# A mixture-of-experts down projection in wide passes: transposed columns and turning them back, or 128 rows and 32-token strips; and the order of the experts

## The reference, cut to what matters

```python
logits = (xf @ router_w) + router_b
top_val, top_idx = lax.top_k(logits, TOP_K)          # 4 of 32 experts
gates = jax.nn.softmax(top_val, axis=-1)
...
h = xb @ w1 + b1                                      # w1[e]: 1024 x 2048
x_glu = jnp.minimum(h[..., :D_FF], 7.0)
x_lin = jnp.clip(h[..., D_FF:], -7.0, 7.0)
act = x_glu * jax.nn.sigmoid(1.702 * x_glu) * (x_lin + 1.0)
return act @ w2 + b2                                  # w2[e]: 1024 x 1024
...
y = einsum("tk,tkd->td", gates, y_assign)             # out = h + y
```

## Time and profile before

| | us |
|---|---|
| runs | 1978.64, 1984.21, 1984.33 |
| median | 1984.21 |
| span of the profiled execution, first to last instruction | 1979.4 |
| TensorE busy in it | 1920.4 |
| prologue, to the first matmul of the first pass | 444.5 |
| 18 narrow passes (n = 128) | 771.2 |
| 14 wide passes (3 of 136, 5 of 144, 3 of 152, 2 of 176, 1 of 192) | 745.9 |
| from the last matmul to the end | 17.8 |

### The profile page before, as it was taken

One profiled execution on the slowest core, in us unless ns is written; L12 is line 12 of the kernel. 1 busy time (PEld: TensorE's weight loads), 2 busy tenths in 40 slices (PEclk: granted clock), 3 DMA queues, 4 the chain that ended last, 5 costly groups with the idle time before them and its releaser, 6 DMA issues.

```text
span 1979.4 us, 34969 instructions
## 1 busy us (share of the span) xinstructions
PE 1920.4 (97%) x12847; PEld 1585.1 (80%) x12848; DVE 1008.8 (51%) x2627; ACT 450.0 (23%) x983; POOL 397.5 (20%) x410
## 2 busy tenths in 40 slices
PE   5999999989999999999999999999999999999996
PEld 3555555458888778888877888999999999999996
DVE  2989983455555455555545555444444444443332
ACT  3166584121111111111111111221222121111111
POOL 3111100012222212212221212222222222221211
PEclk9999999999999999999999999999999999999998
DMA  7000035348999999999999999998888889887651
GB/s 243 1 1 1 10 108 198 127 146 317 344 334 351 340 352 353 344 332 353 341 350 352 351 339 331 324 322 308 303 301 301 301 291 310 306 294 250 220 178 40
DMA packets 237155, 513.10 MB, mean 259 GB/s; under 512 B 11121, under 2 KB 15757, under 8 KB 237104
## 3 DMA queue, kind: packets, MB, share of 16 engines
q1 hardware_dynamic: 215408, 448.89, 62.9%
q0 software_dynamic: 19840, 63.09, 11.8%
q10 hardware_dynamic: 1856, 0.41, 0.1%
HBM read 479.30 MB, written 33.05 MB: 259 GB/s over the span
## 4 chain that ended last, share of the span: by engine, by line
PE 93%; DVE 3%; ACT 1%; issue 1%; DMA 1%; POOL 0%; SPq 0%; ACTq 0%; DVEq 0%; POOLq 0%
PE bank L1178 50%; PE bank L1222 12%; PE bank L1197 12%; PE bank L1395 6%; PE bank L1270 4%; DVE arena L934 2%; PE bank L1306 2%; PE bank L1317 1%; PE bank L1210 1%; PE bank L1211 1%; PE bank L1345 1%; DMA arena<-in_x 1%; PE bank L1564 0%; PE bank L1262 0%; PE bank L1420 0%
## 5 line engine op out<-in xcount | busy, mean ns | idle before, releaser
L1178 PE MATMUL bank<-arena 128*128 128x128 f32 (+5 forms) x8192 | 999.1, 283 | 7.0 <-issue 6.1
L1178 PEld LDWEIGHTS bank<-arena 128*128 128x128 f32 x8192 | 984.9, 191 | 18.9 <-issue 17.7
L379 POOL DMA_INDIRECT arena<-token_rows,idx_q x256 | 246.7, 964 | 667.9 <-PE bank L1178 624.4
L810 DVE TENSOR_SCALAR arena<-bank,b1c 128x256 f32<-128x256 f32 x256 | 123.4, 482 | 404.2 <-PE bank L1178 404.2
L499 ACT ACTIVATE arena<-arena 128x256 f32<-128x256 f32 x256 | 106.6, 417 | 849.1 <-DVE arena L810 849.1
L1222 PE MATMUL bank<-arena 128*128 128x512 f32 x576 | 250.2, 592 | 0.0
L1197 PE MATMUL bank<-arena 128*128 128x144 f32 (+4 forms) x1792 | 246.8, 293 | 3.0 <-ACT arena L503 2.9
L1197 PEld LDWEIGHTS bank<-arena 128*128 128x128 f32 x1792 | 235.3, 190 | 6.2 <-ACT arena L503 6.2
L1222 PEld LDWEIGHTS bank<-arena 128*128 128x128 f32 x576 | 108.1, 190 | 129.1 <-issue 129.1
L934 DVE SCALAR_TENSOR_TENSOR arena<-arena,cols 128x512 f32<-128x512 f32 (+1 forms) x226 | 182.3, 807 | 12.1 <-ACT arena L594 5.1
L855 DVE STREAM_TRANSPOSE arena<-arena 128x256 f32<-128x256 f32 x256 | 87.3, 408 | 193.3 <-DMA arena<-token_rows,idx_q 193.3
(11 more groups left out here) (230 smaller groups left out, 1115.9 us busy)
## 6 DMA issues: line engine op xcount, KB each, us to landing
arena<-in_w SPq DMA_DIRECT2D x192, 2048.0 KB, 12.6
arena<-in_b SPq DMA_DIRECT2D x32, 512.0 KB, 12.5
arena<-in_x SPq DMA_DIRECT2D x16, 512.0 KB, 6.3
token_rows<-arena SPq DMA_DIRECT2D x8, 576.0 KB, 3.2
out<-arena SPq DMA_DIRECT2D x8, 512.0 KB, 6.0
arena<-token_rows,idx_q POOLq DMA_INDIRECT x256
arena<-in_w_in SPq DMA_DIRECT2D x2, 1536.0 KB, 13.2
arena<-in_w_in SPq DMA_DIRECT2D x1, 3072.0 KB, 19.6
```

The source lines that it names most:

```text
L379: pool.indirect_dma_start(out=gath_q[:, g, :], out_offset=None, in_=quads_d, in_offset=bass.IndirectOffsetOnAxis(ap=idx_q[:, g:g + 1], axis=0)
L810: v.tensor_scalar(g1[:, r, :], bank[r][:, 0:SLOTS], b1c[:, m:m + 1], LIMIT, ALU.add, ALU.min).then_inc(g1_ready, 1)
L1178: last = mm(bank[m % 2][:, side * SLOTS:side * SLOTS + n], w1_sb[:, k, lo:lo + P], xT[:, k, 0:n], start=k == 0, stop=k == KD - 1)
```

## The change

`WIDTHS` is reversed, and with it the comparisons that make `tier`. The start at the tier of expert 0, the wrapping and the two laps stay as they are. In `pe_pass` a wide pass computes its first 128 tokens as a narrow one does, and the others in groups of 32, each as four column strips of the array, one for each quarter of the features. Their results and token numbers stand as quarter rows on the partitions (32 tokens x 4 quarters), four such groups at most (`QUADS`), in banks 3 and 7. ScalarE and VectorE handle all four groups in every pass, narrow ones too; GpSimd scatters them as four quarter-row scatters in wide passes only. b2 is loaded a second time as four quarters. `yT`, its copies and the transposes go; the tiny write goes. SyncE's wait for w2's first half is on the first 128 rows' first half and the groups.

```diff
-WIDTHS = [128, 136, 144, 152, 176, 192, 256]
+WIDTHS = [256, 192, 176, 152, 144, 136, 128]
+QG_ROWS = 32
+QUADS = (SLOTS - P) // QG_ROWS
...
+            for j in range(4):
+                sp.dma_start(b2_q[j * QG_ROWS:(j + 1) * QG_ROWS, :],
+                             src[:, j * (D // 4):(j + 1) * (D // 4)].to_broadcast([QG_ROWS, D // 4])).then_inc(b2_in, 16)
...
-                    sp.wait_ge(y_mm, q * KD + (4 * c + 4 - KD))
+                    sp.wait_ge(yt_mm, q * 2 + (c - 1))
+                    if c == 0:
+                        sp.wait_ge(yq_mm, q)
                     load_w2(sp, c, e)
...
+        def quad_bank(g):
+            return bank[3 + 4 * (g // 2)], (g % 2) * (D // 4)
+        def add_quads(pool, g):
+            pool.indirect_dma_start(out=out_q, out_offset=bass.IndirectOffsetOnAxis(ap=idxq_cur[:, g:g + 1], axis=0),
+                                    in_=ytq[:, g, :], in_offset=None, compute_op=ALU.add
+                                    ).then_inc(quad_added, 16)
...
             with pool.Fori(0, n_pass) as q:
+                landed(pool, q)
+                pool.sem_inc(all_landed, 1)
                 pool.wait_ge(idx_q_ready, q + 1)
                 for i in range(4):
                     pool.wait_ge(hid_mm, q * 8 + 5 + i)
                     gather_quads(pool, (2 * i, 2 * i + 1))
+                pool.wait_ge(yq_ready, q + 1)
+                with pool.If(over < len(WIDTHS) - 1):
+                    for g in range(QUADS):
+                        add_quads(pool, g)
+                    pool.reg_add(wide, wide, 1)
                 pool.wait_ge(y_ready, q + 1)
+                add_rows(pool)
...
+            def take_quads():
+                a.wait_ge(yq_mm, q + 1)
+                for g in range(QUADS):
+                    src, at = quad_bank(g)
+                    last = a.activation(ytq[:, g, :], src[:, at:at + D // 4], ACT.Copy, scale=gq_cur[:, g:g + 1])
+                last.then_inc(yq_ev, 1)
+            take_rows(0)
+            take_quads()
+            take_rows(1)
...
+            add_b2(0)
+            v.wait_ge(yq_ev, q + 2)
+            for g in range(QUADS):
+                last = v.scalar_tensor_tensor(ytq[:, g, :], b2_q, gq_cur[:, g:g + 1], ytq[:, g, :], ALU.mult, ALU.add)
+            last.then_inc(yq_ready, 1)
+            add_b2(1).then_inc(y_ready, 1)
...
-            link(v.tensor_scalar(tier, left, float(WIDTHS[0]), None, ALU.is_gt))
-            for n in WIDTHS[1:-1]:
-                link(v.scalar_tensor_tensor(tier, left, float(n), tier, ALU.is_gt, ALU.add))
+            link(v.tensor_scalar(tier, left, float(WIDTHS[1]), None, ALU.is_le))
+            for n in WIDTHS[2:]:
+                link(v.scalar_tensor_tensor(tier, left, float(n), tier, ALU.is_le, ALU.add))
...
-            down(0, range(MT - 1))
-            down(1, range(MT - 1))
-            down(0, [MT - 1])
-            down(1, [MT - 1])
-            for d in range(2, 6):
-                down(d, range(MT))
-                trans_y(d - 2)
-            down(6, range(MT))
-            down(7, range(MT))
-            for d in range(4, KD):
-                trans_y(d)
+            def down_quads(groups):
+                pe.wait_ge(w2_in[1], q16)
+                pe.wait_ge(yq_ev, q + 1)
+                for g in range(groups):
+                    dst, at = quad_bank(g)
+                    lo = P + g * QG_ROWS
+                    for m in range(MT):
+                        for j in range(4):
+                            last = mm(dst[j * QG_ROWS:(j + 1) * QG_ROWS, at:at + D // 4], act[:, m, lo:lo + QG_ROWS],
+                                      w2_sb[:, m, j * (D // 4):(j + 1) * (D // 4)], start=m == 0, stop=m == MT - 1)
+                last.then_inc(yq_mm, 1)
+            down_rows(0)
+            if n == P:
+                pe.sem_inc(yq_mm, 1)
+            else:
+                down_quads(-(-(n - P) // QG_ROWS))
+            down_rows(1)
...
+            pe.wait_ge(spots_ready, 1)
+            mm(bank[2][:, FIRST_Q:FIRST_Q + 2 * QUADS], copies[:], spots[:].rearrange("p h g -> p (h g)"), start=True,
+               stop=True).then_inc(spread_mm, 1)
```

More of the change, by code:

```diff
@@ L94, in hybrid_block @@
         g2_row = part(140, D)
-        ytok = part(144.5, 2, D)
+        ytok = part(144.5, D)
+        ytq = part(148.5, QUADS, D // 4)
         zeros = part(140, D)[0:2, :]
@@ L130, in hybrid_block @@
         b2_rows = part(160, D)
+        b2_q = part(164, D // 4)
         ident = sb("ident", [P, P])
@@ L248, in hybrid_block @@
             "hid_mm", "hid_free", "g1_ready", "sg_ready", "sg_free", "act_ready"))
-        y_mm, yT_ev, yt_mm, yt_ev = sem("y_mm"), sem("yT_ev"), sem("yt_mm"), sem("yt_ev")
-        added = [sem(f"added{i}") for i in range(2)]
+        yt_mm, yt_ev, yq_mm, yq_ev, yq_ready = (sem(n) for n in ("yt_mm", "yt_ev", "yq_mm", "yq_ev", "yq_ready"))
+        added, quad_added, all_landed = sem("added"), sem("quad_added"), sem("all_landed")
         pool_past = sem("pool_past")
@@ L381, in gather_quads, with add_rows @@
                                         ).then_inc(quad_in, 16)
[L383 to L386, removed]
+        def add_rows(pool):
+            pool.indirect_dma_start(out=out2, out_offset=bass.IndirectOffsetOnAxis(ap=idx_cur[:, 0:1], axis=0),
+                                    in_=ytok, in_offset=None, compute_op=ALU.add).then_inc(added, 16)
+        def add_quads(pool, g):
+            pool.indirect_dma_start(out=out_q, out_offset=bass.IndirectOffsetOnAxis(ap=idxq_cur[:, g:g + 1], axis=0),
+                                    in_=ytq[:, g, :], in_offset=None, compute_op=ALU.add
+                                    ).then_inc(quad_added, 16)
         @block.gpsimd
@@ L478, in _, with act_pass, take_rows @@
                     gather_quads(pool, (2 * i, 2 * i + 1))
+                pool.wait_ge(yq_ready, q + 1)
+                pool.sem_inc(pool_past, 1)
+                with pool.If(over < len(WIDTHS) - 1):
+                    for g in range(QUADS):
+                        add_quads(pool, g)
+                    pool.reg_add(wide, wide, 1)
                 pool.wait_ge(y_ready, q + 1)
-                for i in range(2):
-                    pool.wait_ge(added[i], q * 16 + 16)
                 pool.sem_inc(pool_past, 1)
[L483 to L492, removed]
+                add_rows(pool)
+            landed(pool, n_pass)
+        def act_pass(a, q):
             q8 = a.snap(q * 8)
             q2 = a.snap(q * 2)
[L495 to L505, removed]
+            for m in range(MT):
+                a.wait_ge(g1_ready, q8 + m + 1)
+                a.wait_ge(sg_free, q8 + m + 1)
+                a.activation(sg[:, m % 2, :], g1[:, m % 2, :], ACT.Sigmoid, scale=ALPHA).then_inc(sg_ready, 1)
+            def take_rows(b):
                 a.wait_ge(yt_mm, q2 + b + 1)
@@ L508, in take_y @@
                     a.wait_ge(cur_ready, q + 1)
-                    for i in range(2):
-                        a.wait_ge(added[i], q * 16 + 16)
+                    a.wait_ge(all_landed, q + 1)
                 lo = b * HALF
[L512 to L538, removed]
+                a.activation(ytok[:, lo:lo + HALF], bank[4 + b][:], ACT.Copy, scale=gate_cur[:, 0:1]).then_inc(yt_ev, 1)
+            def take_quads():
[7 more added lines that the diff above has]
+            take_rows(1)
         @block.scalar
@@ L778, in _ @@
             with a.Fori(0, n_pass) as q:
-                over = a.value_load(tabI[0:1, ds(q + 64, 1)])
-                act_pass(a, q, over)
+                act_pass(a, q)
         OWN = 32
+        FIRST_Q = SLOTS + 8
         def take_codes(v):
@@ L846, in dve_pass @@
                 if m == 4:
-                    for i in range(2):
-                        v.wait_ge(added[i], q * 16 + 16)
-                    v.tensor_copy(idx_cur[:], idx_pass[:])
+                    v.wait_ge(all_landed, q + 1)
+                    v.tensor_copy(idx_cur[:], idx_pass[:, 0:1])
+                    v.tensor_copy(idxq_cur[:], idxq_pass[:])
+                    v.tensor_copy(gq_cur[:], gq_pass[:])
                     link(v.tensor_copy(gate_cur[:], gate_pass[:]))
@@ L1101, in _ @@
             take_idx(v, idx_next[:]).then_inc(idx_ready, 1)
+            take_idx(v, idxf[:])
             ROUNDS = P // NE
@@ L1184, in pe_pass, with down_rows @@
                 if m == 3:
-                    pe.wait_ge(spots_ready, q + 1)
+                    pe.wait_ge(spots_ready, q + 2)
                     mm(bank[6][:, 16:24], copies[:], spots[:].rearrange("p h g -> p (h g)"), start=True,
                        stop=True).then_inc(spread_mm, 1)
[L1189 to L1211, removed]
-                if d % 4 == 3:
-                    last.then_inc(yt_mm, 1)
-            def down_rows(b, ms):
-                if 0 in ms:
-                    pe.wait_ge(w2_in[b], q16)
-                    pe.wait_ge(yt_ev, q2)
-                for m in ms:
+            def down_rows(b):
```

(3 more changed lines are left out.)

62 lines of the change are left out of this document (35 added, 27 removed).

## The result

The changed kernel takes 2010.1 us in the median of four runs (2005.6 to 2015.0), the kernel before 1983.7: ratio 1.0135, 95% interval 1.012 to 1.0149. It is slower by 26 us, where 14 were forecast. The profiled execution took 2009.94 us. Its span, from the first to the last instruction, is 2008.2, which is 28.8 more than before.

A forecast was written before the change was run, and what follows sets the result against it. TensorE, 93% of the chain of waits, sets the time. Terms -15.7 (wide passes), -2 (tail), +26.4 (jumps), +3 (clock), +2 (laps) sum to +13.7: 1998 us, 0.7% slower, range 1985 to 2013.

The forecast's parts named there:

- between the laps: TensorE's queue between narrow passes and the pass of 192: jump back, skip 256, enter 192; 2 us lost.
- low clock: First pass, after 26 us without a matmul: the clock has fallen; 3 us lost, bounds 0 and 3.4.
- tail: After the last matmul: the last scatter starts 1.8 to 4.7 us later, not 5.6; gain 2, bounds 1 and 4.
- Part 1: Down parts of the 14 wide passes: 256.1 us with 17 groups instead of 271.8; gain 15.7 us.
- rival of slower strips: Groups in wide passes: strips in turn, 13.9 us a group, +177; or slow queue, 7 a group, +60; chance 0.08.
- Part 2: Reversed copy order: six jumps of 4.4 us ahead of the first pass, 26.4 lost; also low clock and the lap turn.
- The bound of 6 for a queued fetch: Jumps ahead of the first pass: upper bound 6 us each if the fetch queues behind w2 and b2 loads.
- The rival of cheap jumps: TensorE's queue before the first pass: prefetcher has the targets, 0.6 us a jump instead of 4.4; 1970 us, chance 0.09.
- the half cheap one: Jumps over the three shorter one-group copies hit fetched instructions: 11.4 us less, 1987 us; chance 0.07.
- At nothing: Inside passes: extra copies, adds, b2 loads, quarter-row scatters and the new wait for landings stay covered, costing no time.

The follow-up runs named there:

- the run with the short copy: Changed kernel with the unused copy for 256 cut to one register instruction, its branch still taken; 1997.7 us in one run.
- one strip after the other: Kernel with the old width order and new down part, each strip doing all eight k blocks before the next; 2091.0 us in one run.
- one more width: Changed kernel with an eighth width, 240, between 256 and 192, used by no expert; 2025.5 us in one run.

## Why the prediction was right, and what was mis-sized

**Sign and mechanism.** Right: the jumps over unused copies outweigh the gain in the wide passes, and the wide-to-narrow order never comes first. The new order alone showed it from one side, the old order with the new down part from the other. The size was not right. The loss on the spans is twice the forecast, and the measured 2010.1 us lies 12 above the 1998, in the upper part of the range, which had let a jump cost 6 us.

| term, us on the span | forecast | measured |
|---|---|---|
| wide passes, at full clock | -15.7 | -17.1 |
| jumps ahead of the first pass | +26.4 | +33.8 |
| between the laps | +2 | +7.9 |
| low clock | +3 | +3.6 |
| tail | -2 | -1.5 |
| prologue | 0 | +2.2 |
| sum | +13.7 | +28.9 |

**Part 1**: -15.0 in the table of the result, -17.1 without the 2.1 us of low clock at the first wide pass. A group takes 3.59 us, two take 7.05, but the switches also lie in the halves around them, 6.96 and 6.97 us where half of the narrow down part is 6.87. A wide pass with one group is 3.78 us longer in its down part than a narrow one, with two 7.24: the 3.8 and 7.3 of the sum were right. Most of what came beyond the forecast is in the hidden parts, 471.9 us at full clock (with the 42.3 of 192 from the run with the short copy) where 473.1 stood. 64 records in 3.59 us are 3.9 times faster than one by one at 0.217. By the share from the Trainium skill ("TensorE: Matmul & The Clock Gate", section "Measured speedup vs the span model"), which is for three column tiles, a group would take an estimated 4.4. The trace doesn't agree for these four, the measurement decides, and the rival of slower strips falls.

**Part 2, jumps ahead of the first pass**: the term that failed by most, 7.4 us. Counted from the prologue's last matmuls, the first pass starts 33.8 us later than before. The one jump in the old trace, 3.8 us, came when all weight loads were done. The bound of 6 for a queued fetch named the case, but the sum took the quiet value for all six. Two of six met the traffic (6.1 and 6.9), and the others take 4.1 to 4.3, with 0.7 each around them. The rival of cheap jumps falls, and so does the half cheap one: the last three, over the copies with one group, take 4.11, 4.10 and 4.31.

**Between the laps**: failed by 6 us and another 2 of low clock, most for its size. It priced two jumps at 3.9 and 3.8 in the fullest stretch of the DMA. At 6.2 and 7.0 the chain of the earlier trace rows gives 7.7. The same bound as above should have been the value here.

**Clock**, forecast 3 at one place: 1.5 there, and 2.1 at the other, where none was forecast.

**Tail**: 1.5 of the 2. The last scatter starts at 1996.96, 5.1 us after the last matmul, behind four others, and not 1.8 to 4.7 after it. The quarter-row scatters take 1.6 us of GpSimd each and more, the upper bound.

**At nothing**: right. The narrow passes keep their 42.8.

**Jumps and loops.** The Trainium skill ("Runtime: NRT & Kernel Launch", section "Instruction fetch mechanics") gives two blocks for a memory of 32 KiB, and TensorE's as 128 KiB. The traces speak for the larger one: a loop of 891 instructions in the trace goes back in 0.24 us (line 1595, at 1379.5). Every jump ahead over a whole copy, 758 instructions or more, took 3.3 us or longer, also on the second lap, though its target had been read on the first, and so did the jump back over all copies. It fits that what lies shortly behind is kept and what lies ahead isn't there; no run shows the memory itself.

**The prologue** was put at nothing. Its last matmuls start at 445.09 instead of 442.94. The later they start, the longer the granted clock had stood at 0.50 in the prologue: none of it with one strip after the other (440.68), 13.6 us before (442.94), 17.0 to 17.1 in the changed kernel and four others (443.31 to 445.53), 20.5 in the old order and with one more width (446.39 and 446.98). The new down part alone is not the cause, as the run with one strip after the other has it too. Why the clock falls more often in one execution than in another, and whether the order has a part in it, is open.

## What to carry to other kernels

Where a program picks one of several long code copies at run time, count the jumps over unused ones: here each cost 4 to 5 us in quiet and 6 to 7 beside full DMA queues, unless long instructions stood in the queue before it, which hid all but 1.6 us of one. Put the copy that runs first in front, the unlikely ones last. A cost read from an event at the end of a trace is that of an idle machine; look up what the same resource carries where the event moves to. Packing 32-column strips paid nearly in full for float32 (3.9 times of 4), with neighbouring instructions on different strips.

## What was not expected

A long branch ahead depends on the DMA traffic: it took 3.3 to 4.6 us with at most 8 GB/s, and 5.8 to 7.3 where it began under weight loads at some 310 to 400 GB/s. The branch of a quarter of a microsecond and those of 4 us and more differ only in how much code lies between them and their target. TensorE starts up to four records of the next strip beside the last of the one before, even when strips are not interleaved: 0.18 us a record instead of 0.216.
